# Product-key experts of one token tile by fetching the selected rows instead of the dense loop

## The reference

```
q      = rms_norm(x) @ w_query            # 8 heads, each two halves of 128
scores = q_half . sub_keys                # 2 x 128 scores a head
top 16 of each half, top 16 of their 256 sums   -> 16 experts of 16384 a head, gates = softmax
a      = gelu(u[expert] . h)              # 8 x 16 = 128 experts a token, rows of 1024
x     += sum over the 128 of gate * a * v[expert]
```

## Time and profile before

| | before |
|---|---|
| median of the runs | 4093.95 us |
| span of the profiled execution | 4092.7 us |
| busy TensorE, VectorE, ScalarE, GpSimd | 91%, 64%, 44%, 4% |
| chain that ended last | in the stretch 3340 to 3420: 97% matmuls |
| DMA | 851 MB, 208 GB/s over the span |

### The profile page before, as it was taken

One profiled execution on the slowest core, in us unless ns is written; L12 is line 12 of the kernel. 1 busy time (PEld: TensorE's weight loads), 2 busy tenths in 40 slices (PEclk: granted clock), 3 DMA queues, 4 the chain that ended last, 5 costly groups with the idle time before them and its releaser, 6 DMA issues. The chain is left out here.

```text
span 4092.7 us, 48110 instructions
## 1 busy us (share of the span) xinstructions
PE 3742.1 (91%) x17280; PEld 3019.1 (74%) x17280; DVE 2600.6 (64%) x3745; ACT 1820.4 (44%) x1842; POOL 175.5 (4%) x171
## 2 busy tenths in 40 slices
PE   8789529999999999975999769999999999999999
PEld 4567427777777777754887558888888888888887
DVE  7326438999999999974531632887777434444443
ACT  1226217777777777751333422344434432222222
POOL 0000020000000000002000000000000000000000
PEclk9899759999999999986999779999999999999999
DMA  7410138999999999985321012344444455555554
GB/s 301 151 53 1 47 130 327 374 377 374 373 379 377 375 375 375 375 333 168 103 93 62 21 67 98 131 179 165 156 171 174 160 199 195 195 183 187 190 181 143
DMA packets 222108, 851.13 MB, mean 208 GB/s; under 512 B 19536, under 2 KB 89424, under 8 KB 146832
## 3 DMA queue, kind: packets, MB, share of 16 engines
q1 hardware_dynamic: 202800, 756.94, 50.8%
q10 hardware_dynamic: 9216, 58.72, 3.5%
q0 software_dynamic: 9952, 33.57, 2.3%
HBM read 745.91 MB, written 103.25 MB: 207 GB/s over the span
## 5 line engine op out<-in xcount | busy, mean ns | idle before, releaser
L1386 DVE TENSOR_TENSOR w_low<-w_raw,w_high 128x2048 fp32r<-128x2048 f32 x399 | 908.8, 2289 | 89.7 <-ACT w_high L1315 82.6
L1315 ACT ACTIVATE w_high<-w_raw 128x2048 fp32r<-128x2048 f32 x399 | 765.2, 1918 | 328.4 <-PE ps L125 181.9
L2337 DVE TENSOR_TENSOR uv_lo<-uv_raw,uv_hi 128x2048 fp32r<-128x2048 f32 x128 | 293.4, 2293 | 655.1 <-ACT uv_hi L2194 654.9
L123 PE MATMUL ps<-w_high,xT_high 128*128 128x512 f32 x1056 | 433.3, 410 | 20.7 <-issue 20.7
L124 PE MATMUL ps<-w_low,xT_high 128*128 128x512 f32 x1056 | 418.2, 396 | 0.0
L125 PE MATMUL ps<-w_high,xT_low 128*128 128x512 f32 x1056 | 417.9, 396 | 0.0
L123 PE MATMUL ps<-h4T_high,uv_hi 128*128 128x512 f32 x1024 | 410.3, 401 | 0.5 <-DVE uv_lo L2337 0.5
L123 PE MATMUL ps<-uv_hi,w_hi 128*128 128x512 f32 x1024 | 405.1, 396 | 2.6 <-issue 2.6
L124 PE MATMUL ps<-uv_lo,w_hi 128*128 128x512 f32 x1024 | 405.0, 396 | 0.0
L125 PE MATMUL ps<-uv_hi,w_lo 128*128 128x512 f32 x1024 | 405.0, 395 | 0.0
L125 PE MATMUL ps<-h4T_high,uv_lo 128*128 128x512 f32 x1024 | 399.4, 390 | 0.0
(11 more groups left out here) (481 smaller groups left out, 6342.0 us busy)
## 6 DMA issues: line engine op xcount, KB each, us to landing
w_raw<-in_w_gate_up SPq DMA_DIRECT2D x267, 1024.0 KB, 6.8
w_raw<-in_w_down SPq DMA_DIRECT2D x132, 1024.0 KB, 6.9
uv_raw<-in_peer_u SPq DMA_DIRECT2D x64, 1024.0 KB, 4.9
uv_raw<-in_peer_v SPq DMA_DIRECT2D x64, 1024.0 KB, 4.9
a_rows<-a_out SPq DMA_DIRECT2D x128, 256.0 KB, 2.1
g_rows<-spread ACTq DMA_DIRECT2D x16, 2048.0 KB, 6.5
qT<-g_rows SPq DMA_DIRECT2D x32, 1024.0 KB, 9.2
qT<-a_rows SPq DMA_DIRECT2D x64, 512.0 KB, 8.1
```

The costliest lines, as they stand in the source:

```text
L123: pe.matmul(out, l_hi, r_hi, start=first, stop=False)
L1315: act.activation(w_hi[:, n % SPLIT, :], w_raw[:, n % RAW, :], ACT.Copy).then_inc(s_wh, 1)
L1386: dve.tensor_tensor(w_lo[:, n % SPLIT, :], w_raw[:, n % RAW, :], w_hi[:, n % SPLIT, :].bitcast(F32), ALU.subtract).then_inc(s_wl, 1)
L2337: dve.tensor_tensor(uv_lo[:, n % 2, :], uv_raw[:, n % 2, :], uv_hi[:, n % 2, :].bitcast(F32), ALU.subtract).then_inc(s_lo, 1)
```

## The change

Token tile 0 leaves the dense loops. The tiles are selected in the order 1, 2, 0, 3; for tile 0 the selected experts' numbers are kept as row numbers, and GpSimd fetches for each of the 128 selections one row per token of u, then of v: 256 indirect transfers of 128 rows. VectorE forms the dot products with a copy of h (one instruction a transfer, with the sum as a second output), ScalarE the gelu in four batches, and VectorE adds weight times row of v to x. The dense u units have 384 moving columns, the v units six banks; there are 96 gate rounds. Rows are used in u units 45 to 63 (74 of them) and in each v unit but the last (3 or 2).

Room for the rows comes from x of tiles 1 to 3 (set aside in DRAM, and loaded again eight units from the end), the keys, the selection's scratch and new buffers: 5, 9, then 10 buffers. The activation buffers fall from three to two and the one-hot slots from six to four. Three of the four first one-hots of a round move to ScalarE, as two instructions each. Gates are loaded once in four v units instead of two, in segments of 1 KB instead of 512 B. A v unit's gate product and its splits are one instruction for both blocks instead of two. A second copy of u in row order is an input.

```diff
     def first_loads(sp):
+        sp.dma_start(x_rest, x_sb[:, 1:TT, :]).then_inc(s_xr, 16)
...
+            for g in range(2 * SEL):
+                if g == MIDDLE_AT:
+                    pool.wait_ge(s_scr, 4 * TT)
+                    pool.wait_ge(s_sel, TT)
+                if g == LATE_AT:
+                    pool.wait_ge(s_gst, 16 * HALVES)
+                if before_of[g] >= 0:
+                    pool.wait_ge(s_rd, before_of[g] + 1)
+                k = g % SEL
+                pool.indirect_dma_start(homes[home_of[g]], None, u_table if g < SEL else v_table,
+                                        bass.IndirectOffsetOnAxis(ap=row_id[:, k:k + 1], axis=0)).then_inc(s_row[home_of[g]], 16)
...
-                        mm = three(pe, ps[:, j, :], hi, lo, h4T[0][:, k, :], h4T[1][:, k, :], k == 0, k == KT - 1)
+                        mm = three(pe, ps[:, j, 0:DENSE], hi, lo, h4T[0][:, k, P:SEQ], h4T[1][:, k, P:SEQ], k == 0, k == KT - 1)
...
-                for at, bank in enumerate(BANKS):
+                for at in range(2 * (TT - 1)):
...
+            def gated_hots(r):
...
+                for q in range(3):
+                    token = (4 * r + q) % P
+                    act.activation(first_hot[:, s, q, :], iota_row[:, :], ACT.Abs,
+                                   bias=selT[:, tile % 2, 3, token:token + 1]).then_inc(s_dist, 1)
+                for q in range(3):
+                    token = (4 * r + q) % P
+                    act.wait_ge(s_dist, 3 * r + q + 1)
+                    act.activation(first_hot[:, s, q, :], first_hot[:, s, q, :], ACT.Relu,
+                                   bias=selT[:, tile % 2, 2, token:token + 1],
+                                   scale=selT[:, tile % 2, 4, token:token + 1]).then_inc(s_hota, 1)
...
+            def row_work(g):
+                row = homes[home_of[g]]
...
+                dve.wait_ge(s_row[home_of[g]], 16 * use_of[g])
+                if g < SEL:
+                    dve.scalar_tensor_tensor(out=row, in0=row, scalar=1.0, in1=h4_s[:, :], op0=ALU.mult, op1=ALU.mult,
+                                             accum_out=row_dot[:, g:g + 1]).then_inc(s_rd, 1)
+                else:
+                    dve.wait_ge(s_rd, g)
+                    dve.scalar_tensor_tensor(out=x_sb[:, 0, :], in0=row, scalar=row_w[:, g - SEL:g - SEL + 1], in1=x_sb[:, 0, :],
+                                             op0=ALU.mult, op1=ALU.add).then_inc(s_rd, 1)
...
             for n in range(2 * NG - 1):
                 low(n + 1)
...
+                if n >= NG:
                     weights(n + 1 - NG)
+                    row_work(rows.pop(0))
+                    weights_low(n + 1 - NG)
+                for g in rows:
+                    row_work(g)
```

More of the change, by code:

```diff
@@ L774, in _ @@
                 next_loads(sp)
+        if keep is not None:
+            @block.gpsimd
+            def _(pool):
+                pool_steps.on(pool)
+                pool.wait_ge(s_h, 1)
+                pool_steps(pool.tensor_copy(keep[:, :], hh[:, 0, :]))
         @block.scalar
@@ L2048, in emit @@
[L2048 to L2057, removed]
@@ L2071, in emit @@
-    BANKS = (2, 3, 4, 5, 6, 7, 0, 1)
-    with nc.Block() as block:
+    s_wf, s_wh, s_wl, s_po, s_add, s_outd, s_xb = (
+        sem(f"peer_{x}") for x in ("weights", "weights_high", "weights_low", "outputs", "added", "stored", "x_back"))
+    s_rd, s_rg = sem("rows_used"), sem("rows_gelu")
+    keys_flat = keysT[:, :, :].rearrange("p a n -> p (a n)")
+    EARLY = [x_sb[:, m, :] for m in range(1, TT)] + [rows_a[:, b, :] for b in range(2)]
+    MIDDLE = [keys_flat[:, b * D:(b + 1) * D] for b in range(2)] + [work[:, b * D:(b + 1) * D] for b in range(2)]
@@ new lines, in emit @@
+    LATE = [rows_c[:, 0, :]]
+    MIDDLE_AT, LATE_AT = 8, 84
+    homes = EARLY + MIDDLE + LATE
+    s_row = [sem(f"row_here{b}") for b in range(len(homes))]
+    home_of, use_of, before_of, last, uses = [], [], [], [-1] * len(homes), [0] * len(homes)
+    for g in range(2 * SEL):
+        b = min(range(len(EARLY) if g < MIDDLE_AT else len(homes) - len(LATE) if g < LATE_AT else len(homes)), key=lambda x: last[x])
+        home_of.append(b)
+        use_of.append(uses[b] + 1)
+        before_of.append(last[b])
+        last[b], uses[b] = g, uses[b] + 1
@@ new lines, in emit @@
+    UNITS_T, UNIT_EXP = 21, 14
+    turns_at = {x: [at + k for k in range(11)] for x, at in enumerate((0, 12, 24, 35))}
+    hots_in = [[1] + [2] * 15 + [1], [2, 2, 2, 1] * 4 + [2, 2], [2, 3] * 6 + [2]]
+    hots_from = (11, 28, 46)
+    rows_in = {45: 2, 46: 4} | {n: 4 for n in range(47, NG)} | {NG + k: 3 if k % 9 else 2 for k in range(NG - 1)}
+    plan, count, at = [[] for _ in range(2 * NG)], [0] * TT, 0
+    for x in range(TT):
+        for n in turns_at[x]:
+            c = min(2, UNITS_T - count[x])
+            plan[n].append(("T", x, c))
+            count[x] += c
@@ new lines, in emit @@
+    for tile in range(TT - 1):
+        assert sum(hots_in[tile]) == P // 4
+        for k, c in enumerate(hots_in[tile]):
+            plan[hots_from[tile] + k].append(("H", at, c))
+            at += c
+    left, at = 2 * SEL, 0
+    for n in sorted(rows_in):
+        c = min(rows_in[n], left)
+        plan[n].append(("S", at, c))
+        at, left = at + c, left - c
+    assert left == 0
+    exp_at, sel_at, scores_at, count = {}, {}, {}, [0] * TT
+    for n in range(NG):
+        for kind, x, c in plan[n]:
+            if kind == "T":
+                if count[x] == 0 and x:
+                    scores_at[n - 1] = x
+                if count[x] <= UNIT_EXP < count[x] + c:
+                    exp_at[n] = x
+                count[x] += c
+                if count[x] == UNITS_T and x != SPARSE:
+                    sel_at[n + 1] = x
@@ new lines, in emit @@
+    assert count == [UNITS_T] * TT
+    rounds_in = [[]] + [[r for kind, x, c in items if kind == "H" for r in range(x, x + c)] for items in plan[:NG - 1]]
+    places = [((), (3,), (2, 6), (1, 4, 7))[len(rounds)] for rounds in rounds_in]
+    turned_before = [sum(y != SPARSE for y in range(x)) for x in range(TT + 1)]
+    BATCH = 32
+    rows_done = [sum(c for items in plan[:n] for kind, _, c in items if kind == "S") for n in range(2 * NG + 1)]
+    gelu_rows_at = {min(n for n in range(2 * NG) if rows_done[n] >= BATCH * (b + 1)): b for b in range(SEL // BATCH)}
@@ L2196, in weights_high @@
             def weights_high(p):
-                for j in range(GROUP):
-                    act.wait_ge(s_wf, 2 * p + j + 1)
-                    act.activation(w_hi[:, p % 2, j, :], wf[:, j, :], ACT.Copy).then_inc(s_wh, 1)
+                act.wait_ge(s_wf, p + 1)
+                act.activation(w_hi[:, p % 2, :, :], wf[:, :, :], ACT.Copy).then_inc(s_wh, 1)
             def spread_round(r):
@@ L2223, in _ @@
                     rounds, early = rounds_in[n], sum(at < 4 for at in places[n])
+                    coming = list(rounds_in[n + 1]) if n + 1 < NG else []
+                    if coming and n not in sel_at:
+                        gated_hots(coming.pop(0))
                     for r in rounds[0:early]:
```

257 lines of the change are left out of this document (148 added, 109 removed).

## The result

The changed kernel takes 3819.69 us, median of 4 runs (3813.43 to 3822.55), against 4094.17 for the kernel before (4093.8 to 4094.44): ratio 0.9327, 95% interval 0.9314 to 0.9341. The forecast was 3791, its range 3728 to 3870. The profiled execution took 3818.46 with a span of 3816.6.

The account below looks back on a forecast made before the run. TensorE's matmuls bound the product-key stage; 371 us less gave a floor of 3722. Adding 50 for v's DMA, 13 for late u, 5 for ScalarE's store wait gave span 3790, plus 1 is 3791 us; range 3728 to 3870.

Parts of the forecast that it names:

- C: Rival: narrower u matmuls do not get cheaper because a weight load must pass each; +45 us, 3836 in all; chance 0.05.
- E: Rival: the saving isn't there because tile 0 goes on being computed; chance 0.01.
- The floor: Whole kernel by TensorE's matmuls alone: 371 us less of the 4092.7 span, 3722 us; v units 8.4 us.
- the DMA term of v: v units: transfers with rows take 9.2 us against TensorE's 8.4, adding 50 us over 63 units.
- A: Rival: TensorE stays the bound, transfers overlap at 423 GB/s, v units 8.4 us, 3735 us in all; chance 0.24.
- B: Rival: DMA at the gather rate or VectorE over budget, 10.0 us a v unit, 3857 us in all; chance 0.22.
- ScalarE's wait for the store: u units with 2.5 rounds: ScalarE waits for the spread gates' store after every eighth round; 5 us in all.
- the 0.6 us a unit: Late u: DMA with rows takes 11.2 us against 10.6, adding 0.6 us on each of 13 units.
- gaps before unit 45: Sign in u that the prediction would be wrong: gaps before the unit where rows begin; no size given.
- the hand-over: Between u and v: a gap of about 2.6 us stays, 2.6 to 5 with one 768-column product included.
- activations behind the rows: Rows' queue may hold up the activations' load, issued 17 us ahead; expected to show with the DMA term, unpriced.
- the 1.4 to 2.5 of the forecast: GpSimd's gathers: each row transfer with some 0.3 us between takes 1.4 to 2.5 us; it fits in v.

Follow-up runs that it names:

- e7: Changed kernel with two spread buffers in turn, gates stored in eight pieces of 16 keys and read back in 512 B segments; ratio 0.9257 to the kernel before.
- e2: Changed kernel fetching only 1 KB of each 4 KB row, with as many gather instructions and dot products multiplied by zero; ratio 0.9129 to the kernel before.
- e3: Changed kernel with VectorE's row instructions on 8 of 1024 columns, all rows still fetched whole; ratio 0.9315 to the kernel before.
- e1: Changed kernel with v's gates loads issued three units ahead of use, behind the activations' load; ratio 0.9297 to the kernel before.
- e8: e7 combined with the edits of e6 and e1; ratio 0.9239 to the kernel before.
- e4: Changed kernel with the dense loops alone, no gathers and no row work, tile 0's experts left out; ratio 0.9122 to the kernel before.
- e6: Changed kernel with v's first two loads of gates and activations issued at units 60 and 61 instead of 62 and 63; ratio 0.9322 to the kernel before.
- e10: e8 with nine rows moved to units 36 to 44 and two gathers instead of three in every fourth v unit; ratio 0.9269 to the kernel before.
- e13: e8 with each 1.5 MB load of gates split into three parts at three units; 3767.1 us, ratio 0.9199 to the kernel before.
- e11: e10 with gates read back in 1 KB segments, the store writing 512 B segments; ratio 0.9268 to the kernel before.

## Why the prediction was right, and where it was not

**Right: what goes.** u matmuls are 0.52 us apart for three, v matmuls 0.68:

```profile
2601.19 0.33 PE L123 MATMUL ps<-h4T_high,uv_hi 128*128 128x384 f32 x1
2601.71 0.33 PE L123 MATMUL ps<-h4T_high,uv_hi 128*128 128x384 f32 x1
...
3420.01 0.39 PE L123 MATMUL ps<-uv_hi,w_hi 128*128 128x512 f32 x1
3420.68 0.39 PE L123 MATMUL ps<-uv_hi,w_hi 128*128 128x512 f32 x1
```

C and E are out by the first pair. The floor was even 0.24 us a v unit too high: a v matmul takes 0.227 us here where the kernel before had 0.233. Scores and turns, priced at 15 us in units 0 to 45, took about 11 (440.2 in e7, less 45 units of 8.32 and 60 rounds of 0.91).

**Right: the DMA term of v, by its mechanism and nearly by its size.** 9.01 us a unit for 9.2, at 362 to 371 GB/s and share 0.96 to 0.99, and e2 and e3 show that the rows' bytes make it, not GpSimd and not VectorE. The mean hides the form: a stalled minority of units beside 43 of 8.2 us. Of the 0.85 us over 8.16, order alone was worth about 0.2 (e1), and loads in thirds took 0.25 from e8; the sum knew bytes only. With the rate of 358 GB/s that the Trainium skill gives for one core ("DMA: Bandwidth & Descriptors", Where 436 GB/s comes from) a unit would have taken an estimated 9.4. The v stages here that fetched whole rows moved 358 to 390 GB/s in windows of 200 to 300 us within v, so the figure is the low end of what was measured and no ceiling. A was wrong on the rate, since 423 GB/s never came with short segments in the mix; B's 10.0 us were the gathers' rate alone.

**Mis-sized: ScalarE's wait for the store, 5 us.** It cost 39: e7, which removes the wait, takes 12 from units 0 to 45 and 27 from 45 to 59. The step took the landing of before (6.5) and 3 us of it as covered, on 13 units only. In the kernel before the wait did not occur: its spreads waited for TensorE alone. After, a unit of u is 2.55 us shorter (10.9 to 8.35), and ScalarE makes three one-hots a round, in two steps each. The groups by line of 3046 to 3172, 25 rounds, give 2.2 us a round, over the 1.3 to 1.9 of the forecast:

```profile
L2296 ACT ACTIVATE first_hot<-first_hot,selT 128x128 f32<-128x128 f32 x75 | 31.5, 486 | 0.0
L2278 ACT ACTIVATE spread<-ps 128x512 f32<-128x512 f32 x24 | 26.1, 1097 | 27.0 <-DMA g_rows<-spread 26.1 <-PE ps L2213 0.9
L2291 ACT ACTIVATE first_hot<-iota_row,selT 128x128 f32<-128x128 f32 x75 | 24.4, 393 | 0.0
```

The cover was ScalarE's slack, so even without gathers ScalarE waited 38.4 us (e4), and with them the landing rose to 12.5. The gaps cost more than their length: from 45 to 59 TensorE is busy 61.6 + 94.4 = 156.0 us with work that takes 147.4, and its granted clock there is 0.97 and 0.91. Late u without this wait is close to free (e7: 149.0 of 147.4), so the 0.6 us a unit that I gave to DMA there were hardly needed: rows were hardly late, VectorE waited 2.9 us for them in all. The prediction had named gaps before unit 45 as a sign of being wrong. They came: 12 of the 39 us lie there.

**Mis-sized: the hand-over, 2.6 us.** The gap was 10.9. The first gates and activations are issued at 3214.34 and stand in the same queue as u's and v's last and first loads while DMA is at 1.02. After the gap a dozen matmuls start 0.43 us apart instead of 0.227 (granted clock 0.81 in that stretch). Issuing the loads earlier (e6) moves the gap and does not remove it; e4 without rows loses 10.9 less over units 59 to 64. I had named this case (activations behind the rows) and priced it at nothing.

**Errors that cancel.** By stretch, the store wait was 34 us more than forecast, the hand-over 7, the start 4, units 59 to 63 and the last unit 2; against it stand 12 less in v, 7 less for DMA in units 45 to 59 and 5 less in units 0 to 45. The sum is 24, from 3793 to the span of 3816.6. So the forecast came this near partly by luck: what was too low adds up to 48.

**GpSimd, VectorE.** The gather instruction took 0.93 to 3.00 us, 1.68 in the median, and a gather with a gap of 0.3 stayed within the 1.4 to 2.5 of the forecast in 64% of cases, below in 19%, above in 17%. That a busy VectorE makes it longer, which the prediction read from 0.93 and 2.23, is borne out by e3 (1.72 to 0.94). Dot products one behind the other start 1.15 us apart, less than the 1.28 taken; the read of the sum (0.081 us) lies beside the next one and adds nothing.

**Open.** The first u unit starts 4 us later than before, in code that the change hardly touches; among the other kernels it started at 2540.2 to 2544.9, so it may be chance, and it wasn't isolated. Nor is it settled why v runs at 363 GB/s in e7 and e10 and at 374 in e8 (e10 and e8 did not run side by side), nor what lets the packets overlap more in e13: only one way of splitting was run. Why a v matmul became cheaper is open too; in e4 it takes 0.227 us at a DMA share of 0.64, above the 0.57 of before, so less traffic is not the reason.

## What to carry to other kernels

When TensorE's work shrinks, every wait that its length covered must be priced again, on each engine: here a buffer stored to memory between two uses went from no wait to one that cost 39 us. Where transfers fill DMA, moving one load mostly changes the name of the wait (e1, e6); what helped here was fewer bytes (e2) and large loads cut and spread evenly (e13). A DMA share near 1 does not say that no more can be moved. And work moved from one engine to another is limited by the second engine's slack in that very unit, not by its mean share.

## What the runs showed of the hardware

- In v the DMA engines at share 0.96 to 1.05 moved 358 to 390 GB/s for nearly the same bytes. A 1.5 MB load split into thirds, one a unit over three units, gave the highest rate with packets of the same length: share rose to 1.05 (e13).
- Halving the segments of the gates (0.39 MB a v unit) to 512 B cost 0.19 us a v unit (e7); longer read segments gave 0.37 back (e11). A packet took 30 ns at 512 B and 52 at 1 KB.
- An indirect gather of 128 rows of 4 KB occupies GpSimd for 0.94 us when VectorE works on 8 columns of each row, and for 1.72 beside multiply-adds of 128x1024 (e3 against the changed kernel).
- A 2 MB store landed in 6.5 us before, in 6.9 without gathers (e4) and in 8.4 in the changed kernel (medians), up to 12.5 beside gathers.
- A multiply with an accumulated sum on VectorE (128x1024, 1.218 us) leaves a second record of 0.081 us, which starts with the next operation.
- A 128x512 matmul in v took 0.227 us instead of 0.233; the cause is open.
